# Attention in wide PSUM regions: one region for a pair's scores, one for its transposes, one bank for the rest

## The reference

```python
def gqa_attend(q, k, v, bias=None, sink=None):
    s = einsum("bqhgd,bkhd->bhgqk", q, k) * ATTN_SCALE
    if bias is not None: s = s + bias
    p = softmax(s)          # with a sink: softmax over the scores and one more column, which is then dropped
    return einsum("bhgqk,bkhd->bqhgd", p, v)

# even: 8 heads A over all 512 + 256 keys, no mask; 8 heads B over a band of 128 before and after,
#       and the 256 keys of the context, with a sink; the context's 256 queries see the context alone
y = concat([oa * silu(ag), ob * silu(bg)]) @ w_out
# odd: 8 heads over 512 keys with a bias by row and column and over the 256 of the context, 512 queries
y = concat([oc, od * silu(dg)]) @ w_out
```

## Time and profile before

| | us |
|---|---|
| median of 3 runs | 2839.03 |
| lowest, highest | 2828.05, 2843.5 |
| the profiled execution | 2840.65 |
| its span in the trace | 2839.0 |
| even attention in it | 2117.1 to 2367.1 |
| odd attention in it | 2628.9 to 2760.8 |

### The profile page before, as it was taken

One profiled execution on the slowest core, in us unless ns is written; L12 is line 12 of the kernel. 1 busy time (PEld: TensorE's weight loads), 2 busy tenths in 40 slices (PEclk: granted clock), 3 DMA queues, 4 the chain that ended last, 5 costly groups with the idle time before them and its releaser, 6 DMA issues.

```text
span 2839.0 us, 34380 instructions
## 1 busy us (share of the span) xinstructions
PE 2594.4 (91%) x13092; PEld 2075.0 (73%) x13092; DVE 1688.6 (59%) x3265; ACT 1133.7 (40%) x2065; POOL 0.2 (0%) x4
## 2 busy tenths in 40 slices
PE   7998899989999899898899899998989997898887
PEld 5876888668888678687786688876866666687655
DVE  6756555455446875565644644477476674499654
ACT  4235443443332332454434423322336664333562
POOL 0000000000000000000000000000000000000000
PEclk9989999989999999898999899998999998899998
DMA  4210033113226422100431223454110000122311
GB/s 146 97 56 16 3 117 107 50 58 105 97 97 214 149 82 97 41 1 17 132 104 38 67 97 97 143 191 150 53 38 16 16 23 23 45 82 67 70 43 45
DMA packets 73505, 219.34 MB, mean 77 GB/s; under 512 B 21248, under 2 KB 21504, under 8 KB 72576
## 3 DMA queue, kind: packets, MB, share of 16 engines
q1 hardware_dynamic: 48384, 176.29, 19.0%
q10 hardware_dynamic: 24960, 40.87, 4.6%
HBM read 215.03 MB, written 2.10 MB: 76 GB/s over the span
## 4 chain that ended last, share of the span: by engine, by line
PE 71%; DVE 16%; ACT 7%; issue 5%; ACTq 1%; DMA 1%; DVEq 0%; SPq 0%
PE bank L575 18%; PE bank L576 17%; PE bank L577 17%; PE bank L789 4%; PE bank L753 4%; DVE mod_part L2500 3%; DVE c_y L2024 3%; PE bank L763 3%; ACT w_hi L534 2%; DVE w_lo L541 2%; PE bank L1207 1%; PE bank L1215 1%; DVE hT L724 1%; PE bank L1153 1%; PE bank L1116 1%
## 5 line engine op out<-in xcount | busy, mean ns | idle before, releaser
L575 PE MATMUL bank<-a_hi,w_hi 128*128 128x512 f32 (+1 forms) x1552 | 624.6, 402 | 45.4 <-ACT a_hi L627 23.7
L576 PE MATMUL bank<-a_lo,w_hi 128*128 128x512 f32 (+1 forms) x1552 | 613.5, 395 | 0.0
L577 PE MATMUL bank<-a_hi,w_lo 128*128 128x512 f32 (+1 forms) x1552 | 613.3, 395 | 0.0
L534 ACT ACTIVATE w_hi<-w_raw 128x1024 fp32r<-128x1024 f32 x334 | 352.3, 1060 | 585.2 <-PE bank L577 488.8
L541 DVE TENSOR_TENSOR w_lo<-w_raw,w_hi 128x1024 fp32r<-128x1024 f32 x334 | 407.4, 1224 | 277.2 <-ACT w_hi L534 276.3
L575 PEld LDWEIGHTS bank<-a_hi,w_hi 128*128 128x128 f32 (+1 forms) x1552 | 295.3, 190 | 133.0 <-issue 47.2
L576 PEld LDWEIGHTS bank<-a_lo,w_hi 128*128 128x128 f32 (+1 forms) x1552 | 295.9, 191 | 64.7 <-issue 3.0
L577 PEld LDWEIGHTS bank<-a_hi,w_lo 128*128 128x128 f32 (+1 forms) x1552 | 295.3, 190 | 65.4
L575 PE MATMUL bank<-b_hi,w_hi 128*128 128x512 f32 x752 | 280.0, 372 | 34.7 <-DVE b_lo L737 23.5
L576 PE MATMUL bank<-b_lo,w_hi 128*128 128x512 f32 x752 | 270.0, 359 | 0.0
L577 PE MATMUL bank<-b_hi,w_lo 128*128 128x512 f32 x752 | 268.1, 357 | 0.0
(11 more groups left out here) (376 smaller groups left out, 3800.1 us busy)
## 6 DMA issues: line engine op xcount, KB each, us to landing
w_raw<-w_tiles SPq DMA_DIRECT2D x334, 512.0 KB, 3.5
mod_raw<-mod_tiles ACTq DMA_DIRECT2D x48, 512.0 KB, 3.5
d_bias<-rpb_rows ACTq DMA_DIRECT2D x16, 224.0 KB, 4.9
hT<-xT ACTq DMA_DIRECT2D x4, 512.0 KB, 11.1
m_in<-memT ACTq DMA_DIRECT2D x2, 1024.0 KB, 4.8
mod_cond<-cond_rows ACTq DMA_DIRECT2D x2, 1024.0 KB, 6.0
out<-hT ACTq DMA_DIRECT2D x8, 256.0 KB, 2.2
ctx_sq<-ctxT ACTq DMA_DIRECT2D x1, 1024.0 KB, 7.7
```

Source lines behind the costliest of these rows:

```text
L534: act.activation(w_hi[:, t % SPLIT, :], w_raw[:, t % RAW, :], ACT.Copy).then_inc(sem("w_rounded"), 1)
L575: pe.matmul(o, wh, hi[:, k, :n], start=k == 0, stop=False)
L576: pe.matmul(o, wh, lo[:, k, :n], start=False, stop=False)
L577: mm = pe.matmul(o, wl, hi[:, k, :n], start=False, stop=k == kc - 1)
```

## The change

The even and the odd attention of the second block get functions of their own (`wide_...`). The first block's attentions stay as they were.

- PSUM is one tensor. Banks 0 to 3 hold the scores of one pair, lane 0 in banks 0 and 1, lane 1 in 2 and 3. Banks 4 to 6 hold the transposes of one pair, side by side. Of the eight, one bank is left for values and gate products by `claim`.
- PE starts a pair's scores when DVE has read the last ones of the pair before (`s_in`), and its transposes when ACT has evicted the pair before's (`pt_in`).
- DVE takes the maximum over all keys at once where there is no mask, and over the two parts apart, each from its own start, where there is; it does both units of a pair and then two divisions.
- ACT evicts a pair's transposes with one instruction where the key tiles are adjacent in the buffer (two where they aren't, heads B); the second unit's exponential stands behind that eviction.
- Gate products run as whole ones: in the even attention eight blocks of 512 columns in pass 1 of six and eight of 256 in pass 3; in the odd one eight blocks in each odd pass.

```diff
+        if n in self.lent:
+            pe.wait_ge(*self.when(*self.lent.pop(n)))
...
+    def borrow(self, pe, first, count):
+        for n in range(first, first + count):
+            assert n not in self.held, n
+            self.held.add(n)
+            if n in self.lent:
+                pe.wait_ge(*self.when(*self.lent.pop(n)))
+            if self.uses[n]:
+                pe.wait_ge(self.sem(f"bank_free{n}"), self.uses[n])
+    def give_back(self, first, count, *event):
+        for n in range(first, first + count):
+            self.held.discard(n)
+            self.lent[n] = event
...
-        banks = [ctx.enter_context(nc.psum_tensor(f"bank{i}", [P, 512], f32)) for i in range(BANKS)]
+        psum = ctx.enter_context(nc.psum_tensor("bank", [P, BANKS * 512], f32))
+        banks = [psum[:, 512 * i:512 * i + 512] for i in range(BANKS)]
...
+        def wide_scores_at(unit):
+            return 512 * SCORES + 2 * S * unit["lane"] + (S + M - wide_width(unit) if len(unit["parts"]) == 2 else 0)
...
+        def wide_turned_at(unit):
+            return 512 * TURNED + (HALF - wide_width(unit) if unit["lane"] == 0 else HALF)
...
+        def wide_scores_pe(pe, key, us, units):
+            if us[0]:
+                v = us[0] - 1
+                pe.wait_ge(*when("s_in", *key, v, len(wide_maxima(units[v])) - 1))
+            c = 0
+            for i in range(len(units[us[0]]["parts"])):
+                for u in us:
+                    _, nk, mms, _ = units[u]["parts"][i]
+                    q, k = mms[0]
+                    at = wide_scores_at(units[u]) + c
+                    pe.matmul(psum[:, at:at + nk], q, k, start=True, stop=True).then_inc(*filled("s", *key, u, i))
+                c += nk
+        def wide_turn_pe(pe, key, j, units, s):
+            if j:
+                pe.wait_ge(*when("pt_in", *key, j - 1))
+            for u in (2 * j, 2 * j + 1):
+                pe.wait_ge(*when("p", *key, u))
+                at = wide_turned_at(units[u])
+                for i, (_, nk, _, _) in wide_parts(units[u]):
+                    c = 0 if i == 0 else units[u]["parts"][0][1]
+                    for n in range(nk // P):
+                        mm = pe.transpose(psum[:, at:at + P], s[:, u % s.shape[1], c + P * n:c + P * n + P], ident)
+                        at += P
+                mm.then_inc(*filled("pt", *key, u))
+        def wide_pe(pe, key, units, s, pt, vt, need, fill, blocks):
+            for event in need:
+                pe.wait_ge(*when(*event))
+            book.borrow(pe, SCORES, 4)
+            n = len(units) // 2
+            ahead = s.shape[1] // 2 - 1
+            pending = None
+            for i in range(n + ahead + 1):
+                if i < n:
+                    wide_scores_pe(pe, key, (2 * i, 2 * i + 1), units)
...
+                if pending is not None:
+                    us = group_of(units, pending)
+                    att_values_pe(pe, key, units, us, pt, vt, [("pt_in", *key, u // 2) for u in us[::2]])
+                    pending = None
+                if i == ahead:
+                    book.borrow(pe, TURNED, 3)
+                if 0 <= i - ahead < n:
+                    wide_turn_pe(pe, key, i - ahead, units, s)
+                    if group_end(units, 2 * (i - ahead) + 1):
+                        pending = 2 * (i - ahead) + 1
+                for _ in range(blocks(i)):
+                    next(fill, None)
+                if i == n + ahead - 1:
+                    book.give_back(TURNED, 3, "pt_in", *key, n - 1)
+            for _ in fill:
+                pass
...
+        def wide_dve(dve, key, units, s, before=None, between=None):
+            ns = s.shape[1]
+            def maxima(u):
+                unit = units[u]
...
+                for j, (c, n, mask, parts) in enumerate(tasks):
+                    for i in parts:
+                        dve.wait_ge(*when("bank_filled", "s", *key, u, i))
+                    m = C("zero").broadcast_to([P, n]) if mask is None else mask
+                    first = unit["sink"] if j == 0 and unit["sink"] is not None else -3.0e38
+                    dve.tensor_tensor_reduce(s[:, u % ns, c:c + n], psum[:, at + c:at + c + n], m, 1.0,
+                                             first, ALU.add, ALU.max, wide_col(u, j)).then_inc(*done("s_in", *key, u, j))
+                dve.wait_ge(*when("s_in", *key, u, len(tasks) - 1))
...
+            for u in range(0, len(units), 2):
+                if before:
+                    before(u)
+                maxima(u)
+                maxima(u + 1)
+                if u:
+                    divide(u - 1)
+                between(u)
+                divide(u)
+                between(u + 1)
+            divide(len(units) - 1)
...
+        def wide_evict_act(act, key, j, units, pt):
+            us = (2 * j, 2 * j + 1)
+            slots = [slot for u in us for slot in wide_slots(units[u])]
...
+            for u in us:
+                act.wait_ge(*when("bank_filled", "pt", *key, u))
+            cuts = [i for i in range(len(slots)) if not i or slots[i] != slots[i - 1] + 1] + [len(slots)]
+            for a, z in zip(cuts, cuts[1:]):
+                op = act.activation(pt[:, slots[a]:slots[a] + z - a, q0:q0 + P],
+                                    psum[:, at + P * a:at + P * z].rearrange("p (k q) -> p k q", q=P), ACT.Copy)
+            op.then_inc(*done("pt_in", *key, j))
+        def wide_act(act, key, units, s, buffer, take, before, between):
+            ns = s.shape[1]
+            n, ahead = len(units) // 2, ns // 2 - 1
+            pt = buffer[:, :, :, :].rearrange("p l k q -> p (l k) q")
+            pending = []
+            for u in range(2 * (n + ahead + 1)):
+                before(u)
+                if u < len(units):
+                    w = wide_width(units[u])
+                    act.wait_ge(*when("max", *key, u))
...
+                    act.activation(s[:, u % ns, :w], s[:, u % ns, :w], ACT.Exp, bias=wide_col(u, 2),
+                                   accum_out=wide_col(u, 3)).then_inc(*done("exp", *key, u))
+                between(u)
+                j = u // 2 - ahead
+                if u % 2 == 0 and 0 <= j < n:
+                    wide_evict_act(act, key, j, units, pt)
+                    if group_end(units, 2 * j + 1):
+                        pending.append((u + 3, 2 * j + 1))
+                if pending and pending[0][0] <= u:
+                    take(act, pending.pop(0)[1])
...
-            return 1 if i % (TT + MT) < TT else 2
+            return KC if i % (TT + MT) in (1, 3) else 0
...
+                t = blocks[0] // KC
+                for p, src_hi, src_lo, n in both(name):
+                    b = claim(pe, p, 0, hold=True)
+                    if n == S:
+                        pe.wait_ge(sem("w_split"), t + 1)
+                    for k in range(KC):
+                        wh, wl = head(w_hi[:, t % SPLIT, :], k), head(w_lo[:, t % SPLIT, :], k)
+                        pe.matmul(b[:, :n], wh, src_hi[:, k, :n], start=k == 0, stop=False)
+                        pe.matmul(b[:, :n], wh, src_lo[:, k, :n], start=False, stop=False)
+                        mm = pe.matmul(b[:, :n], wl, src_hi[:, k, :n], start=False, stop=k == KC - 1)
+                        if k == KC - 1:
+                            mm.then_inc(*(filled(p, 0) if n == S else book.tile_used(p, 0)))
+                            book.release(p, 0)
+                            book.tiles_by[(p, 0)] = t + 1
+                        yield
+                blocks[0] += KC
...
+            c, rest = divmod(u, 2 * (TT + MT))
+            if rest in (4, 8) and c < KC:
+                p, _, sl, n, _ = PARTS[rest // 8]
+                b = bank(act, f"{E_GATE[c]}/{p}", 0)
+                act.activation(even_gate(c)[:, sl], b[:, :n], ACT.Copy)\
+                   .then_inc(*freed(f"{E_GATE[c]}/{p}", 0, also=("e_gate_raw", c, p)))
+        def even_gate_split_act(act, u):
+            c, rest = divmod(u, 2 * (TT + MT))
+            if rest == 9 and c < KC:
+                hi_after(act, f"{E_GATE[c]}/ctx", 0)
         def even_gate_split_dve(dve, u):
-            c = even_gate_ended(u - 1)
-            if c is not None:
-                lo_after(dve, f"{E_GATE[c]}/lat", 0)
+            c, rest = divmod(u, 2 * (TT + MT))
+            if rest == 11:
+                lo_after(dve, f"{E_GATE[c]}/ctx", 0)
...
-            i, rest = divmod(u + 2, KC // 2)
+            i, rest = divmod(u, KC // 2)
             if rest == 0 and 1 <= i <= 2 * CC:
                 name = ODD_GATE[i - 1]
                 b = bank(act, f"{name}/lat", 1)
@@ -1977,10 +2206,14 @@
                     act.wait_ge(*when("c_in", i - 1))
                 act.activation(odd_gate(i - 1), b[:, :], ACT.Copy)\
                    .then_inc(*freed(f"{name}/lat", 1, also=("odd_gate_raw", i - 1)))
-                hi_after(act, f"{name}/lat", 1)
+        def odd_gate_split_act(act, u):
+            i, rest = divmod(u, KC // 2)
```

(8 more changed lines are left out.)

101 lines of the change are left out of this document (74 added, 27 removed).

## The result

Twenty executions of the changed kernel have a median of 2839.36 us (2835.0 to 2844.27), twenty of the kernel before beside them 2834.66 (2828.05 to 2843.5). The ratio is 1.0017, 95% interval 1.0009 to 1.0024: slower by 0.17%, 2.6 to 6.8 us. By the bound of 0.5% that is no change. The prediction said +12 us: the sign is right and the time lies inside its range, but the size is 2.6 times the measured 4.7.

The account below looks back on a forecast made before the run. PE was taken as the bound, busy 98, 95 and 92% of the time. Odd attention +10.7 and even attention +1 made +12 on 2840.65, so 2852 us; forecast range 2842 to 2862 (chance 0.5), 8 in 10: 2828 to 2878.

Parts of the forecast that it names:

- the ledger of the odd attention: Step-by-step sum for the odd attention: start 3.3, periods 1.9, bias transfers 1.0 and end 4.5, together +10.7 us.
- the bias transfers: Odd attention: transfers queue behind the values' eviction, DVE gets the bias late, PE loses 0.5 twice: +1.0 us.
- the end: Odd attention's last values: pass 15's whole gate product, then the last two pairs sharing one region: +4.5 us.
- the periods: Odd attention, two passes each: waits at transposes and gate product make 15.35 in place of 14.97, +1.9 us in five.
- the start: Odd attention: PE idles 10.5 in place of 3.76 until the mask comes, then runs at half clock: +3.3 us.
- Even attention: Heads A -0.3 four times, heads B +0.5 four times, plus its start and end: together +1 us, with wide bounds.
- the real waits of heads B: Even attention: six passes of heads B take 28.65 against terms adding up to 26.2; only there were real waits held.
- Rival 4: The clock falls if waits reach 3 or more in eight head pairs and eight odd periods: +40, 2893 us; chance 0.05.
- 1 (waits hidden): Both attentions: handoffs overlap and PE runs at its own sum, odd periods 14.3; together -21, 2819 us; chance 0.13.
- 2 (no change): Even waits shrink by 2 in each six passes of heads B, -8 to -10 against +10.7: 2841 us; chance 0.14.
- 3 (chains lock): Second exponential waits behind an eviction, DVE divides late; each of 64 passes loses 0.4 more: +25, 2877 us; chance 0.18.
- The prediction's last sentence: ACT's order would upset the sum most: with an early enough values' eviction the odd attention would lose only start and end.

Follow-up runs that it names:

- e1: The changed kernel with the odd attention given back to the old functions, only the even one changed; ratio 0.9995 to the kernel before.
- e2: The changed kernel with the even attention given back to the old functions, only the odd one changed; ratio 1.0012 to the kernel before.
- a1: The changed kernel, but DVE takes heads A's maxima in two instructions in place of one; ratio 1.0010 to the kernel before.
- e3: The changed kernel, but ACT evicts the values' product ahead of the split of gate weights; ratio 0.9999 to the kernel before.
- c4: The changed kernel with whole gate products kept, but ACT evicts the values ahead of the pair's eviction in both attentions; ratio 1.0010 to the kernel before.
- b2: The kernel before the change, with only the column mask's transfer issued early; ratio 0.9978 to the kernel before.
- c1: The changed kernel with half a gate product in every odd-attention pass, ACT's order unchanged; ratio 1.0115 to the kernel before.
- e8: The changed kernel with values evicted before the weight split, first whole gate product in pass 0, early mask, last product moved to pass 16; ratio 0.9990.
- b1: The kernel before, with whole gate products in odd passes in place of four blocks in every pass of the odd attention; ratio 1.0043.
- e4: The changed kernel, but the odd attention's first whole gate product stands in pass 0, not pass 1; ratio 1.0007 to the kernel before.

## Why the prediction was right, and where it was not

**What failed: the ledger of the odd attention, +10.7.** It measured 6.2. Three of its terms were too large, the bias transfers (+1.0, nothing measured), the end (+4.5, at most 2.7) and the periods (+1.9, 1.0), and the start by less. Only the transfers failed as a mechanism.

**What bounds, and where it is lost: right.** The loss is in the odd attention (e1, e2), at the three places named, start, periods and end, and there by the mechanisms named. The changed one took 137.73, 137.19 and 137.39 (this profile, e2, a1), the old one 131.49 and 132.46 (before, e1): the difference of the means is 5.5.

**Start, +3.3 forecast, +2.55 measured.** The idle time was told as 10.5 and is 10.33; the half clock ended at some 2646, 6 us after PE came back at 2639.95, as told. Single profiles scatter here by more than the error: 34.01 and 33.40 before (e1), 34.79 to 36.56 with the change.

**Periods, +1.9 forecast (15.35), +1.0 measured (15.17).** The terms were 14.25 of PE's own, 0.37 at the odd pass's transposes, 0.7 at the gate. They are 0.18 at the transposes (they start at 2684.28, the scores' step of 1.49 is done at 2684.10), 0.87 at the gate (15.17 less e3's 14.30), 0.60 of it shown as idle, and the remaining 14.12 of PE's own. Mechanism and place were right to some tenths; e3 showed that the wait costs.

What the forecast took for PE's waits before, 0.6 in each period, is not spread so. By the earlier trace rows a period is 14.41, and three of the five are; the other two, 15.85 and 15.77, are those with a bias transfer. There ACT issues the transfers, and its next eviction comes after 2.62 of idle time:

```profile
2683.16 0.87 ACT L907 ACTIVATE d_pt<-bank 128x512 f32<-128x512 f32 x2 [2.62 <-PE bank L753]
```

PE's last scores, at 2683.81, wait 0.76 for it. From the first scores to the gate product it is 2.93 (2681.50 to 2684.43) in place of 1.49, which is the 1.4 that the period is longer.

**Bias transfers, +1.0 forecast, nothing measured.** The term that failed outright. The periods with a transfer are as long as the others (15.16 to 15.18), so that the change even takes away what a transfer cost before, some 1.4 a time:

```profile
2682.97 1.45 ACTq L2350 DMA_DIRECT2D d_bias<-rpb_rows  x2
```

This row stands behind the values' eviction in the program, but starts 3.0 ahead of it (2685.99): the transfers are issued while ACT still works through the pair's eviction, the exponential, the split and the values' eviction, all ahead of them in the program. c4 shows the other case, in which ACT had nothing left to do meanwhile: a period 4.2 longer, clock included.

**End, +4.5 forecast, +2.7 measured.** The last step was told as 9.3 and is 9.04. The one before it was told as 15.0 and is 13.48. The prediction gives no terms for the 15.0; it is nearly a whole period, and a period holds the scores of two passes. Here pass 16 has none left (1.49), a slip in counting passes and the largest single error. And of the 2.7 some is the clock's draw in the profile before: against e1's end (21.54) and b2's (21.46) the changed kernel's 22.52 is 1.0 more.

**Even attention, +1 forecast, about +0.2 in the mean of the profiles.** Heads A 31.09 (31.55 told), heads B 28.66 and 28.38 (29.15 told): I added too many waits. PE's idle time in six passes rose from 0.27 to 1.64 with heads A and from 0.73 to 2.4 or 2.7 with heads B, while the rest of them got shorter by 2.1 and 2.0. So what the forecast called the real waits of heads B (28.65 against a sum of 26.2) was for the most part no idle time. The start took 1.9 back in this profile: the wait told as 0.6 is 2.31. The tail at half clock took 2.2 more in four of the profiles. Rival 4 had counted only waits of 3 or more, by the one row of 2.96; the kernel before's own tail (2.19) spoke against that, and so did e1, where the same 2.96 was followed by a lower clock.

**Taken together,** 4.5 of the 12 were terms of the odd attention too large (0.75, 0.9, 1.0 and 1.8), and 0.8 the even one's; by the stages of these two profiles +6.4 would be right, by the means over several 5.7, and the timed executions say +4.7 with 6.8 as the upper end. What remains can't be told from scatter.

**The rivals.** 1 (waits hidden) is what happened in the even periods in part, and in the odd ones once ACT's order was changed: the 14.3 that I gave as its period is e3's 14.29. 2 (no change) names the class that came, but not by its mechanism: heads B gained 0.3 at most where it wanted 2. 3 (chains lock) and, inside the changed kernel's periods, 4 (clock) did not come; c1, e8 and c4 show rival 4's mechanism, behind waits of 2.03 to 3.73. The prediction's last sentence, that the order on ACT would upset the sum most, was the best of it: that order was worth 4.4 in the odd periods (e3) and 5 in the even attention (c4).

**The rule on rotation** (the Trainium skill, Perfetto Trace Analysis, Matmuls: independent matmul groups should rotate through different PSUM banks). As it stands this case neither bears it out nor refutes it. Regions of their own, with half gate products and early evictions of the values, took 120.1 in the odd attention and the rotation 126.85, with the mask early in both: 3.0 of it at the start, 4.0 in the periods, 2.7 of these in the two with a bias transfer. But the order on ACT differs too. The slowest of all were the regions with half products and the change's own order on ACT (c1); next came the rotation with whole products (b1).

## What to carry to other kernels

When two kinds of product share a bank, look which instructions stand ahead of its eviction on the *evicting* engine, and move it up before judging the layout: here that took the wait away with the bank count as it was. A restriction that seems to come with a layout (here whole gate products) should be tested by itself. And at a stage's start, look first for the transfer that all wait for and its place in the queue of issues.

## What the runs showed of the hardware

- The same instructions with the same wait of 2.48 us ran on at half clock for 10 us in one execution (two windows of 0.50); in another (e4) the clock was 0.70 in the first window of 5 us and 0.98 in the second. The stage takes 251.3 or 249.1. Single profiles can't be compared below that.
- In e8 the clock fell behind an idle time of 2.03 (the transposes after it took 2.71 in place of 1.53), and of 2.91 twelve us earlier it had not. In the changed kernel 1.60 and 1.65 with transposes between them left it at full (values 2.81). And 2.96 left it at full in the kernel before, but not in e1 with the same instructions. The length of one wait doesn't decide alone.
- ACT's queue issued transfers up to 3.0 us ahead of an instruction of ACT that stands in front of them in the program. With four such instructions unfinished the issue cost nothing (15.16 to 15.18). With one it held ACT up: 4.23 us for four transfers in c4, idle time 3.95; 2.95 in the kernel before, idle time 2.62, period 1.4 longer.
- Width was worth nothing on DVE (0.96 for 768 columns against 0.69 + 0.42, period the same). On ACT it was worth 0.12 us in an odd period and 0.35 in six passes of heads A.
- Eight transfers ahead of one in ACT's queue of issues held it up by 8 us (2623.45 to 2631.51).
